# Beginning the next stage of a two-layer trunk with the first half of the tokens, and halving the staging while doubling the split blocks

## The reference

```
layer 0:  gate, u = split(x @ w_in)            # 2048 -> 2 x 2048
          u = causal_conv4(u) + b;  r, i = sigmoid(block-diagonal gates of u)
          h = linear recurrence over the tokens
          x = LN(alpha*x + (gelu(gate) * h) @ w_out)
          x = LN(alpha*x + (relu(x @ w1)**2) @ w2)      # 2048 -> 8192 -> 2048
layer 1:  q, k, v = split(x @ w_qkv); partial rotary; causal attention, 16 heads
          x = LN(alpha*x + attention @ w_out)
          x = LN(alpha*x + (relu(x @ w1)**2) @ w2)
```

## Time and profile before

| | |
|---|---|
| median of 3 runs | 2128.06 us (2125.64 to 2128.58) |
| the profiled execution | 2126.73 us, its span 2124.8 us |
| TensorE busy | 2110.1 us, 99% of the span |
| VectorE busy | 1304.2 us, 61% |
| ScalarE busy | 973.9 us, 46% |
| DMA | 406.14 MB, mean 191 GB/s |

### The profile page before, as it was taken

The page is one execution under the profiler, slowest core; times in us unless marked ns, Lnnn a source line. Parts: engine busy times, 40 slices in busy tenths (PEclk is TensorE's granted clock), DMA queues, the critical chain, the costliest instruction groups (busy, mean ns, idle before and its releaser), DMA issues.

```text
span 2124.8 us, 31006 instructions
## 1 busy us (share of the span) xinstructions
PE 2110.1 (99%) x10956; PEld 1800.3 (85%) x10956; DVE 1304.2 (61%) x1240; ACT 973.9 (46%) x1092; POOL 29.8 (1%) x22
## 2 busy tenths in 40 slices
PE   9999999999999999999999999999999999999999
PEld 8898888888888888888888888888888888888887
DVE  6769665665645554565767666676655645645655
ACT  5596444434434443443544445344434434433443
POOL 0000010000000000000100000010000000000000
PEclk9999999999999999999999999999999999999999
DMA  8656665666566666666555556666666666567652
GB/s 281 189 186 195 230 207 184 190 194 191 183 201 182 197 193 191 191 192 188 163 167 171 166 167 219 197 199 180 201 193 189 193 192 190 183 199 228 193 191 101
DMA packets 210497, 406.14 MB, mean 191 GB/s; under 512 B 12496, under 2 KB 18896, under 8 KB 209392
## 3 DMA queue, kind: packets, MB, share of 16 engines
q1 hardware_dynamic: 209840, 400.80, 60.9%
q10 hardware_dynamic: 576, 4.19, 0.5%
HBM read 402.85 MB, written 2.10 MB: 191 GB/s over the span
## 4 chain that ended last, share of the span: by engine, by line
PE 97%; DVE 1%; issue 0%; ACT 0%; DMA 0%; SPq 0%; ACTq 0%; DVEq 0%
PE ps L393 40%; PE ps L385 34%; PE ps L382 17%; PE ps L629 1%; PE ps L627 1%; PE ps L628 1%; PE ps L523 0%; PE ps L642 0%; PE ps L495 0%; PE ps L496 0%; PE ps L494 0%; DMA wst<-in_rg_w_in_dram 0%; PE ps L617 0%; DVE bnst L1114 0%; DVE f L1107 0%
## 5 line engine op out<-in xcount | busy, mean ns | idle before, releaser
L900 DVE TENSOR_TENSOR wl<-wst,wh 128x1024 fp32r<-128x1024 f32 x743 | 901.6, 1222 | 649.1 <-ACT wh L660 646.9
L660 ACT ACTIVATE wh<-wst 128x1024 fp32r<-128x1024 f32 x743 | 779.5, 1058 | 896.4 <-PE ps L393 469.2
L385 PE MATMUL ps<-xin,wh 128*128 128x512 f32 x3072 | 1058.2, 395 | 3.9 <-issue 1.3
L382 PE MATMUL ps<-xin,wl 128*128 128x256 f32 x3072 | 821.5, 278 | 0.0
L393 PE MATMUL ps<-wh,hid 128*128 128x512 f32 x2560 | 694.8, 389 | 0.0
L385 PEld LDWEIGHTS ps<-xin,wh 128*128 128x128 f32 x3072 | 563.1, 188 | 122.3 <-issue 3.1
L382 PEld LDWEIGHTS ps<-xin,wl 128*128 128x128 f32 x3072 | 577.2, 188 | 16.9
L393 PEld LDWEIGHTS ps<-wh,hid 128*128 128x128 f32 x2560 | 479.8, 188 | 99.5
L393 PE MATMUL ps<-wl,hid 128*128 128x512 f32 x1280 | 404.4, 389 | 0.0
L393 PEld LDWEIGHTS ps<-wl,hid 128*128 128x128 f32 x1280 | 240.3, 188 | 49.8
L910 DVE TENSOR_TENSOR e<-e,ps 128x1024 f32<-128x1024 f32 x32 | 39.1, 1221 | 48.6 <-ACT e L669 48.6
(11 more groups left out here) (126 smaller groups left out, 661.6 us busy)
## 6 DMA issues: line engine op xcount, KB each, us to landing
wst<-in_mlp_w_dram SPq DMA_DIRECT2D x512, 512.0 KB, 3.8
wst<-in_moba_w_qkv_dram SPq DMA_DIRECT2D x96, 512.0 KB, 4.3
wst<-in_rg_w_in_dram SPq DMA_DIRECT2D x63, 512.0 KB, 4.1
wst<-in_rg_w_out_dram SPq DMA_DIRECT2D x32, 512.0 KB, 4.9
wst<-in_moba_w_out_dram SPq DMA_DIRECT2D x32, 512.0 KB, 4.9
f<-in_x_dram SPq DMA_DIRECT2D x8, 256.0 KB, 8.5
wst<-in_rg_gate_a_w_dram SPq DMA_DIRECT2D x4, 512.0 KB, 4.1
wst<-in_rg_gate_x_w_dram SPq DMA_DIRECT2D x4, 512.0 KB, 3.9
```

Of the source, the lines that this page charges most:

```text
L382: mm = pe.matmul(dst[:, n, 0:T], wl[:, s, w], src[:, c, 0, :], start=False, stop=(c == NC - 1))
L385: pe.matmul(dst[:, n, :], wh[:, s, w], src[:, c, :, :], start=(c == 0), stop=False)
L660: act.activation(wh[:, off % SPLITS, :], wst[:, kb, :], ACT.Copy).then_inc(wh_done, 1)
L900: dve.tensor_tensor(wl[:, off % SPLITS, :], wst[:, off % BLOCKS, :], wh[:, off % SPLITS, :], ALU.subtract).then_inc(wl_done, 1)
```

## The change

Six edits, made together.

1. `last_token_turn`: all 8 blocks serve token half 0 first, then all 8 serve half 1. Between blocks 3 to 6 of half 1, TensorE transposes half 0 of the normalised result, one group of four chunks at a time (`norm_unit(n, 0, g)`), into banks 6 and 7.
2. `begin_with_first_half`: the next stage's first turn begins with blocks 0 to 5 (`BEGUN`), high part of the weights only, on the first 128 tokens: matmuls of 2 x 128 columns. In between, half 1 is transposed (`norm_unit(n, 1, g)`). `begun_turn` then does the rest: for blocks 0 to 5 the second 128 tokens (2 x 128 columns) and the low part of the weights, for blocks 6 and 7 the usual matmuls. `keep_warm` is gone from this place, and the order by twos stands at block 6.
3. 4 staging blocks and 8 split blocks in place of 8 and 4; `AHEAD` is 7, and with it `START`, `LATE`, `NEXT`. The two small buffers `e1`, `e2` move into `f2`, and a scratch area of the build is halved.
4. Groups 0 and 1 of half 0 are normalised by VectorE, 2 and 3 by GpSimd. ScalarE and VectorE do gain, bias and split by token half and group of four chunks, in a new order.
5. ScalarE issues the loads of the first two weight blocks; SyncE's loads 4 to 7 wait for a staging slot.
6. ScalarE issues the two stores of column group 0.

```diff
-SPLITS = 4
-AHEAD = 4
+STAGE = 4
+SPLITS = 8
+AHEAD = 7
...
+BEGUN = 6
...
                 if b is not None:
-                    sp.wait_ge(wl_done, b - (BLOCKS - 1))
+                    sp.wait_ge(wl_done, b - (STAGE - 1))
...
+                if kb > 1:
+                    load_block(first[kb], kb, None if kb < STAGE else kb)
...
-                for kb in range(HELD):
...
-                    for kb in range(HELD, BLOCKS):
+                    for kb in range(BLOCKS):
...
+                            if n < 3 and 3 <= kb < 3 + NG:
+                                norm_unit(n, 0, kb - 3)
...
+            def norm_unit(n, h, g):
+                if h == 0:
+                    bank = 6 + g % 2
+                    if g < 2:
+                        pe.wait_ge(z_dve, Z_DVE * n + g + 1)
+                    else:
+                        pe.wait_ge(z_pool, 2 * n + g - 1)
+                        pe.wait_ge(v_done, STEPS * n + g - 1)
+                else:
+                    bank = 4 + g
+                    pe.wait_ge(z_dve, Z_DVE * n + g + 3)
+                    if g >= 2:
+                        pe.wait_ge(v_done, STEPS * n + g + 1)
+                for q in range(GROUP):
+                    c = g * GROUP + q
+                    mm = pe.transpose(ps[:, bank, q * P:(q + 1) * P], res[:, h, c * P:(c + 1) * P], ident[:, :])
                 mm.then_inc(xt_done, 1)
+            def begin_with_first_half(n, b, free):
+                pe.wait_ge(psum_free, free - 1)
+                for kb in range(BEGUN):
+                    pe.wait_ge(h0_ready, NG * n + kb // 2 + 1)
+                    pe.wait_ge(wh_done, b + kb + 1)
+                    for c in range(kb * KCH, (kb + 1) * KCH):
+                        for m in range(GROUP):
+                            w = slice(c % KCH * COLS + m * P, c % KCH * COLS + (m + 1) * P)
+                            pe.matmul(half_of(ps[:, m, :], 0), wh[:, c // KCH % SPLITS, w], xin[:, c, :, 0:P],
+                                      start=(c == 0), stop=False)
+                    if kb >= 3:
+                        norm_unit(n, 1, kb - 3)
+                norm_unit(n, 1, 3)
+            def begun_turn(n, b, ready):
+                for kb in range(BLOCKS):
+                    if kb >= BEGUN:
+                        pe.wait_ge(h0_ready, NG * n + kb // 2 + 1)
+                    pe.wait_ge(pair_ready, ready + (kb + 1))
+                    pe.wait_ge(wl_done, b + kb + 1)
...
+                        for m, low in (by_twos if kb == BEGUN else one_by_one):
...
-                for done, count, times in ((psum_free, free + 2, 3), (ln_var, 2 * n + 2, 3),
-                                           (ln_root, 2 * n + 2, 2)):
-                    pe.wait_ge(done, count)
-                    keep_warm(times)
-                for k in range(4):
-                    norm_pair(n, k)
-                keep_warm(3)
+                begin_with_first_half(n, b + 2 * BLOCKS, free + 2)
...
+            first = cols_of(rg_w_in[0], D)
+            for q, landed in enumerate((first_half, stage_full[0])):
+                act.dma_start(wst[:, 0, q * COLS:(q + 1) * COLS], first[0, :, q, :]).then_inc(landed, 16)
+            act.dma_start(wst[:, 1, :].rearrange("p (k n) -> p k n", k=KCH), first[1]).then_inc(stage_full[1], 16)
...
+                        act.wait_ge(out_act, h + 1)
+                        act.dma_start(out[0, h * P:(h + 1) * P, 0:COLS], res[:, h, 0:COLS]).then_inc(stored, 16)
...
                 inverse(0)
-                splits(b, BLOCKS, BLOCKS + 2)
+                for g0 in range(2):
+                    z(0, g0)
+                splits(b, BLOCKS, BLOCKS + 3)
+                split_norm(0, 0)
+                splits(b, BLOCKS + 3, BLOCKS + 4)
+                split_norm(0, 1)
                 add_half(1)
+                split_norm(0, 2)
                 inverse(1)
...
```

172 lines of the change are left out of this document (88 added, 84 removed).

## The result

The kernel takes 2115.2 us after the change (median of 4 runs, 2114.61 to 2115.64), against 2127.11 of the runs of the kernel before made beside it (2125.64 to 2128.58). The ratio is 0.9943, with a 95% interval of 0.9931 to 0.9955: 11.9 us faster. The profiled execution has a span of 2113.4 us where the one before has 2124.8.

A forecast was written before the change was run, and what follows sets the result against it. TensorE's instruction stream was taken to bound the kernel. Gains of 10.9 at three boundaries, 0.7 at the start and 0.9 at the end sum to 12.5 us, taking the median from 2128.06 to 2115.6 us, range 2111.8 to 2121.

The forecast's parts named there:

- The boundaries: At the three LayerNorms inside the trunk, from token turn's end to next turn's end: 3.63 us gained each, 10.9 together.
- the sum of 26.89: Predicted length in us of one boundary after the change, from transposes, half matmuls, pairs and a wait; 30.52 before.
- The wait of 0.2: At a boundary, TensorE waits 0.1 to 0.3 us, taken as 0.2, for half 1's first normalised piece.
- The cut of 512 into two: In the begun turn, cutting a 512-column matmul costs 13 ns by the trace, 0.64 us a boundary; 2.5 ns by the skill.
- What has to be ready: At a boundary, normalised, scaled and split pieces of both halves are ready before TensorE asks for them.
- The cover for half 1: Before `begun_turn`, half 1's first piece is split at 7.3 us, wanted at 7.8: thinnest cover, 0.5 us.
- The staging: In the long runs, four staging and eight split blocks keep the 12-block depth; costed at 0.
- The start: At the first loads, SyncE and ScalarE issuing side by side shorten two TensorE waits: 0.7 us gained, at most 1.4.
- The end: After the last matmuls, half 1's addition no longer starts 0.55 us late, one store issue saves 0.35: 0.9 us together.
- The late boundary: Rival at the boundaries: half 1's cover gone or first normalised piece late, 1.8 us lost each, giving 2121; chance 0.15.
- slow half matmuls: Rival at the boundaries: matmuls of two 128-column runs take as long as 512 columns, giving 2146; chance 0.06.
- starved splits: Rival in the long runs: four staging blocks cannot keep up if landings average 9 us, about 2265; chance 0.04.

The follow-up runs named there:

- e10: Changed kernel with no blocks begun: half 1 is waited for before the next stage's first turn, filler in the hole; 2130.84 us.
- e4: Kernel before with only the new staging, 4 staging and 8 split blocks; 2127.9 us, ratio 1.0003 to the kernel before.
- e8: Changed kernel with VectorE normalising all of half 0 and GpSimd none of it; 2114.66 us.
- e7: Changed kernel with four begun blocks in place of six; 2121.39 us.
- e11: Kernel before with only ScalarE issuing the first two weight blocks, 8 staging blocks, no slot waits; one run, 2129.7 us.
- e1: Changed kernel with SyncE issuing all first weight blocks again, slot waits kept; 2114.44 us.
- e6: Changed kernel with SyncE issuing all eight stores again; 2115.13 us.
- e5: Changed kernel with 5 unused matmuls before the first transposes and 5 after, in place of 3 and 3; one run, 2113.41 us.
- e2: Changed kernel with 4 unused matmuls before the first transposes and 5 after, in place of 3 and 3; 2114.44 us.
- e9: Changed kernel with SyncE issuing the first weight blocks and VectorE normalising all of half 0; 2113.68 us.
- e3: Changed kernel with SyncE issuing the first weight block again and ScalarE only the second; 2115.24 us.

## Why the prediction was right, and where it was not

The forecast was 2115.6, the time 2115.2. The mechanism held: TensorE's stream bounds the kernel, the gain is at three boundaries and comes from the begun half (e10), and the staging changes nothing (e4). But two terms were off in opposite directions, and the nearness of the total owes something to that luck. So it does to the starting point: the forecast took 12.5 from a median of 2128.06, while the kernel before, run beside the changed one, had 2127.11; as differences, 12.5 us stand against 11.9 by the medians and 11.4 by the spans.

- **The boundaries, 10.9 predicted, 12.9 measured.** The step that was mis-sized is the sum of 26.89. A group of transposes costs 0.41 to 0.43, not 0.48: eight of them 3.35, not 3.86. With 17.35 for the 144 half matmuls and 5.61 for the pairs that is the 26.31 measured. The 0.48 was what was left of the turn behind the hole when all 64 pairs were taken at 0.347, but some of them ran slower: where the pairs do run at that pitch, a group and eight pairs take 316.75 - 313.54 = 3.21 in the timeline before, so the group 0.43. The wait of 0.2 for the first normalised piece of half 1 did not come: VectorE begins to normalise 3.03 us after the token turn, 307.74 - 304.71, where 3.15 was reckoned, and it does a piece in 0.48 when GpSimd is idle (e8), where 0.73 was taken from a stretch in which both worked. Half matmuls at 0.120 and pairs at 0.351 were as predicted or near it. The third boundary before was longer than assumed (30.76), by slower pairs in its turn.
- **The cut of 512 into two.** The trace shows 3.83 for 32 matmuls of 256, so the row's 0.120 held. The figure of the Trainium skill (TensorE: Matmul & The Clock Gate, Back-to-back issue gap), 0.109, by which the prediction estimated 1.6 us more gain in all, does not agree with it.
- **What has to be ready.** ScalarE's four small pieces take 1.50, as estimated. The cover for half 1 was put at 0.5 and is 0.18: its split is ready 7.22 us after the token turn, where 7.3 was reckoned, but TensorE comes at 7.40 and not at 7.8, because the transposes ahead cost less. It held, but e7 shows what it is made of: with 16 matmuls fewer ahead of it, TensorE waits 1.54.
- **The staging, 0 predicted.** e4 measures a ratio of 1.0003. The order of the token turn, also at 0, was not tested by itself; its timeline shows no wait.
- **The start, a gain of 0.7 predicted, a loss of 2.0 measured.** This term failed, in sign too. The step took 0 to 1 us at each of two waits from the issue time saved, and took for granted that what is issued first lands as it did. e11 shows the edit alone costing 2.4 us at the first stretch, e1 shows it undone. 0.84 is the first piece of x, which is now issued at the same moment as the two half blocks, and lands later when they are (e1 and e11; that they share the DMA engines' time is the likely reason, and was not shown apart); the other 1.11 up to the second block is TensorE's first matmuls at the wide spacing. The saved microsecond is real at the landing (8.8 for 9.79), but the path to the second block no longer led through its load: it goes through x's second piece on TensorE and ScalarE. So the wait for the block (1.2 now) did not go away.
- **The end, 0.9 predicted, 0.5 measured.** The 0.55 of the late addition came. The 0.35 of an issue saved did not: by e6 stores from ScalarE change nothing.
- **The range.** Its lower end, 2111.8, is 0.3 above what its own terms give (2113.0 less 1.5 is 2111.5). Nothing hangs on it.
- **The rivals.** The late boundary, slow half matmuls and starved splits all had their sign in the rows (a wait, a pitch over 0.14, waits for wl in long runs); none is there.

Open remains what sets the spacing of the first matmuls, that is, when TensorE leaves the lower level at which all fourteen profiled executions begin (1.11 or 1.12 us for the first four transposes). Idle time ahead of it may play a part: e5, with 0.20 instead of 0.59 idle ahead of the transposes, is narrow where e2 is wide, once each. How long the wide stretch lasts differs too: about 10.7 us is its end after the change, about 13.8 in e11. And the wide one goes with the late piece in seven kernels of eight, without it in one of six. But e1 and e9 have the same stream and differ, so one profiled execution each does not settle what decides. The Trainium skill (TensorE: Matmul & The Clock Gate, What's actually happening) says that the number of matmuls at the low clock varies from run to run of one kernel; the pair e1 and e9, two kernels with the same start, agrees with that. Nor is it settled why some turns take 22.20 us and others 22.58.

## What to carry to other kernels

When a normalisation stands between two stages of a matmul-bound kernel, finish the half of the data that is independent first and let the next stage begin on it with what needs only that half; the hole of 6.4 us was filled at a price of 13 ns a cut matmul. How much is begun decides it: six blocks cover the normalisation by 0.18 us, four leave a wait of 1.5. Issuing first loads from a second engine is no free gain: here it delayed just the piece that the first matmul waits for. Look where that piece lands, not where it is issued, and follow what stands between a landing and the matmul that uses it.

## What the runs showed of the hardware that was not expected

- VectorE's scaling of 128x512 float32 takes 0.48 us alone (1.91 for four) and 0.69 to 0.73 beside GpSimd doing the same. GpSimd takes 2.33 a piece beside a mixture of VectorE's work (two splits of weights, 2.36 of the 9.32 us, then addition, statistics and normalising), and 3.25 where VectorE split three blocks of weights, 3.48 of the 6.49 us. The Trainium skill (SBUF — State Buffer, Who interferes with whom) has the two engines share a pair of ports, and says that a VectorE instruction with two SBUF inputs, as the split of weights is, contends with a GpSimd instruction that reads SBUF; the rows fit it, though no run here took the splits alone away.
- The three first weight loads issued by ScalarE beside SyncE's delayed the landing of SyncE's first: in all eight kernels that had them x's first piece takes 3.7 to 3.9 us from issue to landing and TensorE transposes it at 4.48 to 4.74 us; in the six others it is 2.8 to 3.0, and 3.55 to 3.78.
- TensorE's first matmuls ran at one of two spacings, 1.24 or 2.27 us for 2560 columns (to 0.01), with a granted clock of 1.00 in the profile either way, and nothing in between in fourteen kernels. All fourteen begin at the lower of the two levels. Of the eight with ScalarE's loads seven were wide, of the six others one.
- A turn of 64 pairs takes 22.20 or 22.58 us (22.29 or 22.67 for q, k and v) and nothing in between, with no wait in the trace: outside the boundaries four turns are long before and after the change, one in e2, five in e1 and e3.
